# Silu of the conditioning vector in columns, low parts of the first weights on VectorE, first output tile inside the last attention slots

## The reference, cut to what matters

```
def rms_norm(x, g): return x * rsqrt(mean(x*x) + EPS) * g
def ada_modulation(c, w, b, n): return split(silu(c) @ w + b, n)      # silu(c) = c / (1 + exp(-c))

shift, scale, gate = ada_modulation(c, a_ada_w, a_ada_b, 3)
u = rms_norm(h, a_norm_g) * (1 + scale) + shift
q, k, v, z = split(u @ a_w_in, 4)                  # layer A: 8 heads, differential, causal
q, k = rms_norm(q), rms_norm(k)
o = (softmax_1 - lam * softmax_2) @ v              # per head, ALiBi
o = rms_norm(o, a_subln_g) * 0.8 * silu(z)
h = h + gate * (o @ a_w_out)
kv_shift, kv_scale = ada_modulation(c, kv_ada_w, kv_ada_b, 2)
k_s, v_s = split((rms_norm(h, kv_norm_g) * (1 + kv_scale) + kv_shift) @ w_kv, 2)
shift, scale, gate = ada_modulation(c, b_ada_w, b_ada_b, 3)
u = rms_norm(h, b_norm_g) * (1 + scale) + shift
q, z = split(u @ b_w_in, 2)                        # layer B: 16 heads, window 128, sinks
o = sliding_window_attention(rms_norm(q), k_s, v_s) * silu(z)
h = h + gate * (o @ b_w_out)
```

## Time and profile before

| what | us |
|---|---|
| runs, median of 3 | 1236.7 (1235.08 to 1238.17) |
| profiled execution, its time | 1240.81 |
| profiled execution, its span | 1239.0 |
| TensorE busy | 1141.4 (92%) |
| VectorE busy | 730.4 (59%) |
| ScalarE busy | 668.9 (54%) |
| GpSimd busy | 172.7 (14%) |
| TensorE's share of the chain that ended last | 81% |

### The profile page before, as it was taken

One profiled execution on the slowest core, in us unless ns is written; L12 is line 12 of the kernel. 1 busy time (PEld: TensorE's weight loads), 2 busy tenths in 40 slices (PEclk: granted clock), 3 DMA queues, 4 the chain that ended last, 5 costly groups with the idle time before them and its releaser, 6 DMA issues.

```text
span 1239.0 us, 18959 instructions
## 1 busy us (share of the span) xinstructions
PE 1141.4 (92%) x5920; PEld 883.9 (71%) x5920; DVE 730.4 (59%) x2344; ACT 668.9 (54%) x2039; POOL 172.7 (14%) x305
## 2 busy tenths in 40 slices
PE   1478999999999999999978999689999999998997
PEld 1356777777777777777756888568877788787886
DVE  7676767767677676767663545545555555555221
ACT  3665565656666565655652555546656666664010
POOL 1510011111111010111100111121111111110212
PEclk9688999999999999999988999889999999996999
DMA  9621222323222223222213332300111111123342
GB/s 367 207 79 49 84 77 83 95 68 95 68 85 76 102 72 94 84 77 84 69 41 140 119 121 67 119 18 27 43 48 39 40 39 49 42 57 119 119 136 85
DMA packets 51125, 107.92 MB, mean 87 GB/s; under 512 B 5584, under 2 KB 18000, under 8 KB 50896
## 3 DMA queue, kind: packets, MB, share of 16 engines
q1 hardware_dynamic: 51024, 106.70, 27.1%
HBM read 89.90 MB, written 16.78 MB: 86 GB/s over the span
## 4 chain that ended last, share of the span: by engine, by line
PE 81%; DVE 7%; issue 5%; ACT 4%; DMA 2%; POOL 1%; POOLq 0%; DVEq 0%; SPq 0%; ACTq 0%
PE ps_p L517 15%; PE ps_p L519 13%; PE ps_p L518 13%; PE ps_s L549 6%; PE ps_o L599 5%; PE ps_p L690 4%; PE ps_p L691 4%; PE ps_p L692 4%; PE ps_o L659 3%; PE ps_t L612 3%; PE ps_s L643 2%; PE ps_t L675 2%; PE ps_o L714 2%; PE ps_o L575 1%; PE ps_t L704 1%
## 5 line engine op out<-in xcount | busy, mean ns | idle before, releaser
L517 PE MATMUL ps_p<-w_hi,u_hi 128*128 128x512 f32 x768 | 338.7, 441 | 19.9 <-DVE u_lo L1047 19.9
L519 PE MATMUL ps_p<-w_hi,u_lo 128*128 128x512 f32 x768 | 305.7, 398 | 0.0
L518 PE MATMUL ps_p<-w_lo,u_hi 128*128 128x512 f32 x768 | 304.7, 397 | 0.0
L517 PEld LDWEIGHTS ps_p<-w_hi,u_hi 128*128 128x128 f32 x768 | 147.1, 192 | 84.2 <-ACT gbuf L777 28.6
L519 PEld LDWEIGHTS ps_p<-w_hi,u_lo 128*128 128x128 f32 x768 | 146.6, 191 | 33.5
L518 PEld LDWEIGHTS ps_p<-w_lo,u_hi 128*128 128x128 f32 x768 | 147.9, 193 | 17.6
L826 ACT ACTIVATE e<-e,negm 128x256 f32<-128x256 f32 (+7 forms) x128 | 98.3, 769 | 98.6 <-DVE negm L1100 97.5
L998 DVE TENSOR_TENSOR w_lo<-raw,w_hi 128x512 fp32r<-128x512 f32 x120 | 82.5, 695 | 92.5 <-ACT w_hi L750 92.3
L451 POOL TENSOR_SCALAR gbuf<-gbuf 128x128 f32<-128x128 f32 (+1 forms) x96 | 36.6, 381 | 569.5 <-ACT gbuf L777 569.5
L549 PE MATMUL ps_s<-kT,qT 64*128 64x512 f32 (+3 forms) x384 | 90.2, 547 | 7.2 <-DVE negm L1100 4.6
L750 ACT ACTIVATE w_hi<-raw 128x512 fp32r<-128x512 f32 x128 | 79.0, 629 | 11.8 <-DMA raw<-w_a 7.9
(11 more groups left out here) (161 smaller groups left out, 2039.1 us busy)
## 6 DMA issues: line engine op xcount, KB each, us to landing
adabuf<-ada_w SPq DMA_DIRECT2D x48, 512.0 KB, 3.9
raw<-w_a SPq DMA_DIRECT2D x80, 256.0 KB, 3.9
raw<-w_b SPq DMA_DIRECT2D x48, 256.0 KB, 3.1
ada_in<-ada_w SPq DMA_DIRECT2D x7, 1024.0 KB, 14.3
x_in<-x SPq DMA_DIRECT2D x8, 512.0 KB, 7.3
oa_scratch<-gbuf SPq DMA_DIRECT2D x64, 64.0 KB, 1.6
e<-oa_scratch SPq DMA_DIRECT2D x8, 512.0 KB, 3.6
stage<-x SPq DMA_DIRECT2D x8, 512.0 KB, 5.1
```

The lines of the kernel that those rows point to most:

```text
L517: pe.matmul(o, u_hi[:, c, t], w_hi[par][:, c, :], start=(c == 0), stop=False)
L518: pe.matmul(o, u_hi[:, c, t], w_lo[par][:, c, :], start=False, stop=False)
L519: mm = pe.matmul(o, u_lo[:, c, t], w_hi[par][:, c, :], start=False, stop=(c == KD - 1))
```

## The change

Silu of c is computed on 128x8 (the columns of c stand in `prm` now, at `C_VEC`), copied along the rows of `pT`, transposed on TensorE into `ps_s` and copied to `c_silu` by ScalarE. The load of c as 128 rows goes. GpSimd no longer makes low parts; VectorE makes those of chunks 0 to 3 behind modulation rows 12 to 15 and those of chunks 4 to 7 behind `x_low(0)`. Chunks 4 to 7 of the first unit get buffers of their own in `e0` (`raw_chunk`), so that their loads wait for nothing. The roots of x move from behind rows 5 and 9 to behind rows 3 and 8, the last lambda steps to behind row 6.

In both layers rows 0 and 1 of the attention's output are loaded in slot 1 of the last five, as soon as the last projection is done, into `late`, which lies over `u_lo`; all row loads of the output go there, and each is of eight pieces of 512 bytes a partition instead of one of 4 KB. Tile 0 is transposed in slot 2 (into `ps_p`), split on ScalarE and VectorE in the same slot, its first half made in slot 3 behind the gate and ahead of the last product with the values; tile 1 is transposed behind that, and tile 0's second half made in slot 4. The output loop begins at its step 2 on TensorE and ScalarE, at 1 on VectorE.

```diff
@@ SyncE
+                    if not live(0) and i == 1:
+
+                        sp.wait_ge(S.proj, units * NT)
+                        for k in range(2):
+                            sp.wait_ge(S.st[k], 16 * ((units - 1) * NT // 2 + 1))
+                            sp.dma_start(rows_in_u(k), groups(o_dram[k * P:(k + 1) * P, :], P)).then_inc(c_o[k], 16)
                     if not live(0) and i < 4:
                         for c in (2 * i, 2 * i + 1):
                             load_chunk(units + 1 + unit0, c, w_src[units + 1, :, c, :])
-                    if not live(0) and i == 4:
-                        sp.wait_ge(S.pt, units * (UNIT_CHUNKS if is_a else NT))
-                        for k in range(2):
...
-            sp.dma_start(c_silu, c_row).then_inc(s_crow, 16)
@@ GpSimd
-            for c in range(KD):
-                pool.wait_ge(w_hi_done, c + 1)
-                pool.tensor_tensor(w_lo[0][:, c, :], raw[:, c % RAW, :], w_hi[0][:, c, :].bitcast(F32),
-                                   ALU.subtract).then_inc(w_lo_done, 1)
@@ TensorE
+            def out_rows(n0, n):
+                m = n0 + n
+                pe.wait_ge(c_o[n % 2], 16 * (m // 2 + 1))
+                at_least(pe, c_lo, 2 * m)
+                for d in range(KD):
+                    mm = pe.transpose(rows_psum(n)[:, d * P:(d + 1) * P], rows_in_u(n)[:, d, :], ident[:, :])
...
+            pe.wait_ge(s_silu, 4)
+            for d in range(KD):
+                mm = pe.transpose(ps_s[:, d * P:(d + 1) * P], pT[:, d * P:(d + 1) * P], ident[:, :])
+            mm.then_inc(s_ctr, 1)
@@ ScalarE
+            def transposed(n0, n):
...
+                    if not live(0) and i in (2, 4):
+                        transposed(n0, i // 2 - 1)
...
-            act.activation(e0[:, 0, :], c_silu, ACT.Exp, scale=-1.0).then_inc(s_cexp, 1)
+            act.activation(cexp[:, :], prm[:, C_VEC:C_VEC + KD], ACT.Exp, scale=-1.0).then_inc(s_cexp, 1)
@@ VectorE
+            dve.tensor_copy(groups(pT[:, :], P), csil[:, :].unsqueeze(2).to_broadcast([P, KD, P])).then_inc(s_silu, 1)
...
+                if j >= ADA0 - RAW:
+                    split_lo(0, j - ADA0 + RAW, 0)
...
             x_low(0)
+            for c in range(RAW, KD):
+                split_lo(0, c, 0)
             x_modulate(1)
```

More of the change, by code:

```diff
@@ L541, in gate_rows, with out_half, attn_a @@
                 mm.then_inc(g_mm, 1)
-            def attn_a(S, units, gate):
+            def out_rows(n0, n):
[4 more added lines that the diff above has]
+                    mm = pe.transpose(rows_psum(n)[:, d * P:(d + 1) * P], rows_in_u(n)[:, d, :], ident[:, :])
+                    if d % 4 == 3:
+                        mm.then_inc(c_tr, 1)
+            def out_half(n0, unit, n, h):
+                m = n0 + n
+                at_least(pe, c_y, 2 * (m - 1) + h + 1)
+                for c in range(KD):
+                    if h == 0 and c % 4 == 0:
+                        pe.wait_ge(c_lo, 2 * m + c // 4 + 1)
+                    if n == 0:
+                        w_ready(pe, unit + h, c)
+                    hi, lo = rows_t(n, 0)[:, c, :], rows_t(n, 1)[:, c, :]
+                    pe.matmul(ps_p[:, h, :], hi, w_hi[h][:, c, :], start=(c == 0), stop=False)
+                    pe.matmul(ps_p[:, h, :], hi, w_lo[h][:, c, :], start=False, stop=False)
+                    mm = pe.matmul(ps_p[:, h, :], lo, w_hi[h][:, c, :], start=False, stop=(c == KD - 1))
+                mm.then_inc(c_mm, 1)
+            def attn_a(S, units, gate, n0, unit_out):
                 def scores(u, it, n, part):
@@ L605, in slot @@
                     part_of_projection(range(4, 7))
+                    if not live(0) and i == 2:
+                        pe.wait_ge(S.ez, units * NT)
+                        pe.wait_ge(S.qn, units * NT)
+                        out_rows(n0, 0)
                     if i >= 3:
@@ L730, in output @@
                         mm.then_inc(k_tr, 1)
[L731 to L732 removed]
+                    if n1 < NT:
+                        out_half(n0, unit, n1, 1)
                     if with_next and s in (NT + 1, NT + 2):
@@ L979, in _ @@
                     x_normalise(k, n)
-            for c in range(KD):
+            for c in range(RAW):
                 split_hi(0, c, 0)
@@ L1174, in slot @@
                     split_for(u, i, par, live, units, U_A)
+                    if not live(0) and i in (2, 4):
+                        transposed(y_done, i // 2 - 1)
                     if first and i >= 2:
@@ L1269, in output @@
                 chain = 0
-                for s in range(NT + (4 if with_next else 1)):
+                for s in range(1, NT + (4 if with_next else 1)):
                     n1, n2, n3, n4 = s - 1, s - 2, s - 3, s - 4
```

186 lines of the change are left out of this document (100 added, 86 removed).

## The result

| | median us | runs | profiled execution | its span |
|---|---|---|---|---|
| before | 1236.88 | 4 (1235.08 to 1238.17) | 1240.81 | 1239.0 |
| after | 1218.21 | 4 (1216.09 to 1219.78) | 1219.1 | 1217.2 |

The ratio is 0.9847, 95% interval 0.9832 to 0.9862: 18.7 us faster, where 16.9 was forecast (1219.8). So the total is right. Its parts are not all right (5.5, 7.7 and 3.7 were forecast for the beginning and the two tails), and one choice in the change costs time.

What follows compares the result with a forecast made beforehand. TensorE bounds the long middle, untouched; it stands still at the beginning and in both attention tails. Gains 5.5 + 7.7 + 3.7 = 16.9 take the median from 1236.7 to 1219.8, range 1215 to 1228.

Steps and rivals of the forecast that it cites:

- The beginning: First 56 us: earlier c_silu and silent GpSimd bring u_hi of tile 1 at 44.5 instead of 50.09; gain 5.5.
- the landing of rows 12 and 13: Beginning: 10.74 MB must have landed for these modulation rows; at 392 GB/s from 2.0 us that is 29.4.
- Rival 3: Beginning: slower transfers, the last row pair lands at 32.0 instead of 29.4, the whole takes 1222.4; chance 0.05.
- my reading of the long rows: Beginning: modulation rows take 2.28 us instead of 1.29 while GpSimd computes low parts; with it silent nothing lengthens them.
- Tail of layer A: End of layer A's attention: tile 0's rows loaded and multiplied earlier, normed row's transposes at 675.5 instead of 683.20; gain 7.7.
- the hole for the transposes: Layer A's tail: tile 0's 1.9 us of transposes fit where TensorE would wait for the softmax until 648.62.
- the high end's own clause: Layer A's tail: gain up to 9.2 if filling the hole at 647 keeps the clock up through the gate product, 1.5 less.
- Tail of layer B: End of layer B's attention: the half of tile 1 starts at 1147.4 against 1151.08; gain 3.7, ends 1.9 and 5.2.
- (1): Tails of both layers: tile 0's first half runs at the lower clock, -2.4 and -1.8, so 1224.0; chance 0.20.
- (2): Output row loads: small pieces of 512 bytes run at half rate, so 1222.4; chance 0.10.
- (4): Beginning and tails: VectorE's extra low parts and TensorE waiting for last splits eat the gain, 13 us of waits, 1236.7; chance 0.03.
- (5): Both tails: clock stays low through tile 0 and tile 1's first half, 28.8 more less 16.9, 1248.6; chance 0.02.

Runs made afterwards that it cites:

- e11: The changed kernel run once more, the same program with nothing altered: median 1219.59 us, ratio to before 0.9861.
- e3: The changed kernel with GpSimd again computing the eight low parts of the first weights instead of VectorE: median 1214.83 us, ratio to before 0.9790.
- e7: The changed kernel with output rows of tiles 2 to 7 loaded as one 4 KB piece a partition: median 1219.24 us, ratio to before 0.9849.
- e5: The changed kernel with the first four weight chunks loaded behind the last modulation rows, all splits and low parts behind tile 0's modulation: 1218.0 us, ratio to before 0.9841.
- e2: The kernel before with only the changed tails of both layers, beginning as before: median 1221.0 us, ratio to before 0.9843.
- e1: The kernel before with only the changed beginning, both tails as before: median 1233.1 us, ratio to before 0.9958.
- e12: The changed kernel with both halves of tile 0 behind the last product with the values, in both layers: median 1213.82 us, ratio to before 0.9809.
- e9: The changed kernel, residual and tile 2 rows requested ahead of the last store, layer A's last splits ahead of the square: 1214.84 us, ratio to before 0.9829.

## Why the prediction was right, and where it wasn't

**The beginning: 5.5 forecast, 4.1 in the first profile, 3.1 in e11.** The chain was right step by step: four rows and four low parts took 7.24 us (7.3 forecast), from the end of smod to u_hi of tile 1 it was 7.67 (7.6 forecast). Wrong was one term, the landing of rows 12 and 13: 29.4 forecast, 30.93 and in e11 31.93 measured (the start of row 12, which waited for it). The rate was not at fault (390 GB/s from 2 to 33 us in the kernel after too); the step took the queue as strictly in order, so that 10.74 MB sufficed. At 390 GB/s 28.9 us move 11.3 MB: some half a megabyte more than the step counted, an estimate from these two numbers. That transfers queued behind had moved as well is the likely reason; no run isolates it. By the Trainium skill's 358 GB/s ("DMA: Bandwidth & Descriptors", "Where 436 GB/s comes from") the landing would be 32.0, an estimate; it came near that time, but the measured rate, 390, is not the page's. Rival 3 (2.9 for this term) came about by half in the first profile and nearly in full in e11, though not by a slower queue.

That GpSimd's silence is worth something was my reading of the long rows. e3 refutes it for the sum: rows are long beside GpSimd, yet smod is ready within 0.1 us of the same time. I had costed VectorE's extra low parts (2.45) and never asked what leaving them on GpSimd would give.

**Tail of layer A: 7.7 forecast; 8.9 and 6.9 measured like for like.** With the early fall, as in the profile of before, A went from 54.4 to 45.5 and 45.6 (e7, e5), with the late one from 51.3 to 44.4. Right were the hole for the transposes, no wait for weights, the wait of the half of tile 1 (1.0 forecast, 0.98 in after, e2, e7 and e11), and the sum that waits for the residual (3.5 forecast, 3.6 measured). The miss is the high end's own clause, that a filled hole keeps the clock up through the gate product. Granted clock 15 to 23 us after the projection, first of the kernel before, then of e7, whose tail lies 3.9 earlier:

```profile
644.00:648.00 4.00, 2.88 (x14) 2.68 (x14) 2.65 (x9) 3.05 (x8) 0.00 (x0) 0.71 0.01 1
648.00:652.00 4.00, 3.38 (x19) 3.14 (x20) 3.31 (x9) 2.13 (x6) 0.00 (x0) 0.72 0.27 73
```
```profile
640.00:644.00 4.00, 3.79 (x24) 3.54 (x22) 2.57 (x9) 2.97 (x7) 0.00 (x0) 0.71 0.00 0
644.00:648.00 4.00, 3.30 (x26) 3.02 (x27) 3.89 (x7) 2.89 (x7) 0.00 (x0) 1.00 0.24 67
```

After the same fall TensorE is busy for 3.79 of four us instead of 2.88 and the clock stays up; before, it fell again. The gate product took 1.95 in e7 against 3.57, 1.6 less; the term lacked 1.2. One execution of the old tail and two of the new (e5, e7) show this, so it is likely, not settled. Sure is that a stretch at 0.50 around the waiting first half is in both profiles with the old tail (before, e1) and in none of the eleven with the new.

**Tail of layer B: 3.7 forecast, 5.7 in nearly all profiles** (B 32.5 to 32.6 in nine, 31.2 and 27.3 in two). Order and absence of waits were right. The price was not: I gave the gate product 3.4 us at the low clock (from its start to the first half it took 2.4, from 16.54 to 18.93 behind the projection) and the half a slow beginning, and the clock was back at 1.00 about 18 us after the projection, inside the gate product, as in e11 (projection until 1097.47):

```profile
1110.00:1114.00 4.00, 4.00 (x20) 4.00 (x20) 3.80 (x9) 2.72 (x7) 0.00 (x0) 0.50 0.40 113
1114.00:1118.00 4.00, 4.00 (x24) 3.75 (x24) 1.94 (x5) 3.16 (x6) 0.00 (x0) 0.82 0.23 84
```

In layer B the old tail hides the clock, the new one doesn't (in layer A the old one did not hide it either, 54.4 and 51.3): B is 38.3 and 38.4 in before and e1, though e1's clock came back early, because the first half waited for its rows until 24.5 us in either. With the waits gone B is work alone, and its length is the clock's (27.3 with none lost).

**The sum.** Like for like: about 4.0, 8.9 and 5.7, 18.6, beside 18.7 and 18.1 in the medians (1237.67 less 1219.59); with layer A's 6.9 of the late fall it is 16.6, so the close agreement is in part a choice of the pair. Of forecast and result 1.5 too much at the beginning, 1.2 and 2.0 too little in the tails cancel in part: that the total came within 1.8 us of 16.9 is partly luck. The profiled pair's 21.8 holds some 3 us by which the clock fell early in one and late in the other. That the gains belong to the median, as waits that every execution has, and not to the profiled difference fits: the medians differ by 18.7.

**The rivals.** (1) First halves of tile 0 at the low clock: in no profile with the new tail. (2) Small pieces: no (e7, for tiles 2 to 7). (3) In part, see above. (4) No wait for the last splits in the second half, but they do hold product and residual back: 1 to 2 us, not 13. (5) Refuted: no stretch at 0.50 from the first half of tile 0 to the end of A or of B in any profile with the new tail.

## What to carry to other kernels

When arithmetic goes out of the way of a load queue, price the landing with what is queued behind it as well, and ask first which bytes ahead aren't wanted yet: moving 1 MB brought 2 to 3 us. Before work is put into a waiting engine, look at what is queued behind the next product on the other engines: here the half ahead of a product that had its operands cost 2 us in layer A (e12, e9). And compare stretches at an equal fall of the clock, from more than one execution: once waits are gone, the clock's luck is a term of its own (some 3 us between the two first profiles, and up to 4 us outside the tails).
